# Adding up a norm's squares on GpSimd instead of VectorE, in a two-layer decoder trunk

## The chip, the core and the metric

One of the eight cores of a Trainium2 chip runs the whole program. The metric is the device time of one execution, in microseconds (us), taken as the median of several runs. The engines are called as in the profile: PE (TensorE), PEld (its weight loads), ACT (ScalarE), DVE (VectorE), POOL (GpSimd) and SP (SyncE, which only issues transfers here).

## What is computed

Two layers (`DEPTH` = 2) of a decoder trunk with model width 1024 are run on 592 tokens at once: 64 of the sample group, 16 meta tokens and 512 of the prompt. Cut to what matters here:

```python
def rmsnorm(x, g):
    xf = x.astype(jnp.float32)
    y = xf * lax.rsqrt(jnp.mean(xf * xf, axis=-1, keepdims=True) + EPS)
    return (y * g.astype(jnp.float32)).astype(x.dtype)

def swiglu(x, wg, wu, wd):
    return (jax.nn.silu(x @ wg) * (x @ wu)) @ wd

# one layer
h = h + 0.5 * swiglu(rmsnorm(h, norm_ffn1), ffn1_gate, ffn1_up, ffn1_down)
x = rmsnorm(h, norm_mix)
...                     # four mixers (convolution, retention, GLA, attention), gated and merged
h = h + merged @ w_out
h = h + 0.5 * swiglu(rmsnorm(h, norm_ffn2), ffn2_gate, ffn2_up, ffn2_down)
```

Each layer has three norms. Each needs, for every token, the sum of the squares of 1024 channels.

## The kernel before

The residual stream `hT` lies in SBUF as eight tiles (`KD` = 8) of 128 channels by 592 tokens. For a norm, ACT squares one tile into `tmp[:, 0, :]`; DVE adds this to `ssum` (128 by 592, float32); after eight tiles PE multiplies `ssum` by a matrix of ones, which adds over the partitions, and ACT makes the inverse root from it. `tmp[:, 0, :]` is one buffer: ACT may square tile m+1 only when the sum of tile m is done. Three semaphores carry this: `squared` (ACT has squared), `squares_summed` (the add is done) and `sum_cleared` (DVE has set `ssum` to zero).

All float32 operands of PE are split into a high and a low part (`x_hi`, `x_lo`, `w_hi`, `w_lo`); ACT writes the high parts, DVE the low ones, and PE makes three products of each pair. The gate and up projections are done as a fast matrix product of seven block products over halves of the operands, so for them sums and differences of halves of `hT` are formed as well (`T1`, `T2`, `T3`, `T4`, and the plain halves `B11`, `B22`, `B21`). This is done tile by tile as soon as a tile of `hT` is there: tiles 0 to 3 by `first_tile`, tiles 4 to 7 by `second_tile`, followed for the second FFN of a layer by `fourth` and the low parts of `T3`, `B21` and `T4`. The same engines also prepare, between the tiles, the weights for the first block products of the next stage (`first_operands`).

There are five places where tiles are squared for a gate and up projection:
- the prologue, on the input `h_in`, before the loop over layers (the add is at L2482)
- in each layer, `residual(l, 8, U_OUT, ...)`: `hT` is updated by the output projection (L2001, directly from PSUM), units of one weight block per tile, called the out stage below (adds at L1834)
- in each layer, `residual(l, 16, U_DOWN2, ...)`: `hT` is updated by the down projection of the second FFN (L1998, then L2001), three weight blocks per tile, called the down stage (adds at L1834). After layer 1 it is the last thing the kernel does, and nothing uses its squares.

The third norm of a layer, in front of the mixers, has its adds at L1974 and is not touched.

Every engine runs its own list of instructions in order and waits on semaphores. In the prologue ACT waits for `squares_summed` of the tile before, in front of the high part of the next tile; in `residual` it waits in `tile_added`, in front of the last weight unit of the next tile. PE waits for all eight adds in `norm`, which stands behind two block products of the first pair of the FFN (L1240). POOL's list in this kernel holds transfers alone: constants at the start, then one that waits for `brow` (`bias_row_made`, L569), caches and tables of the mixers within the loop, and at the end of a layer's list the parameters of the next layer (L661), which wait for the last low part `T4` of the second FFN.

Of the kernel before, what the change touches and what calls it, by code (L numbers as in the profile page):

```python
# [23 lines left out]
ALU = mybir.AluOpType  # L24
# [6 lines left out]
KD, KF = D // P, FF // P  # L31
# [29 lines left out]
KH = KD // 2  # L61
# [35 lines left out]
def parts(L, f, name, k):  # L97

    return L * sum(map(len, PARTS)) + f * len(PARTS[0]) + PARTS[f].index((name, k)) + 1
# [17 lines left out]
P_GAIN = 0  # L117
# [39 lines left out]
def split_cols(ap):  # L157

    return ap.rearrange("p (h t) -> p h t", h=2)


def build(nc, h_in, wstream, wlow, params, vbias, cache_k, cache_v, page_table, st_ret, st_gla,
# [9 lines left out]
    with ExitStack() as ctx:  # L172
        def sem(name):
            return ctx.enter_context(nc.semaphore(name))
# [7 lines left out]
        def keep(name, shape, dt=F32):  # L182
            nonlocal at
            t = place(name, shape, dt, at)
            at += -(-4 * int(np.prod(shape[1:])) // 32) * 32
            return t
# [11 lines left out]
        tmp = keep("tmp", [P, 2, T])  # L198
# [3 lines left out]
        ssum = keep("ssum", [P, 2 * NB * (CK - 1 + NT)])[:, 0:T]  # L202
# [142 lines left out]
        def pair(p):  # L345
            return ps[:, 2 * p:2 * p + 2, 0:HALF]
# [11 lines left out]
        sum_cleared = sem("sum_cleared")  # L358
        squared = sem("squared")
        squares_summed = sem("squares_summed")  # L360
# [193 lines left out]
        def _(pl):  # L554
            def load_values(l, p):

                for b in (2 * p, 2 * p + 1):
                    for pg in range(PAGES):
                        page = pl.value_load(pages[0:1, b * PAGES + pg:b * PAGES + pg + 1], min_val=0, max_val=POOL - 1)
                        pl.dma_start(vpage[:, b % 2, pg, :], cache_v[ds(l * POOL + page, 1)].rearrange("a p n -> (a p) n")).then_inc(values_loaded[b % 2], 16)  # L560

            pl.dma_start(prm[:, :], params[0][:, 0:NP_ - P]).then_inc(params_loaded, 16)
            pl.dma_start(pages[:, :], page_table).then_inc(consts_loaded, 16)
            pl.dma_start(ones[:, :, :], c_ones).then_inc(consts_loaded, 16)
# [1 line left out]
            pl.dma_start(coef[:, 0:2], c_coef).then_inc(consts_loaded, 16)  # L566
            pl.dma_start(rb[0:33, :], rel_bias).then_inc(consts_loaded, 16)
            pl.dma_start(bucket[0:33, :], c_bucket).then_inc(consts_loaded, 16)
            pl.wait_ge(bias_row_made, 3)  # L569
            pl.dma_start(scratch, brow[:, :]).then_inc(bias_row_stored, 16)  # L570
            pl.wait_ge(bias_row_stored, 16)
# [5 lines left out]
            with pl.Fori(0, DEPTH) as l:  # L577
# [77 lines left out]
                pl.dma_reset(range(nums[0], nums[-1] + 1))  # L655
                pl.sem_clear(range(nums[0], nums[-1] + 1))
                pl.sem_inc(mixers_open, 1)

                pl.wait_ge(x_parts, parts(l, 1, "T4", 3))
                pl.sem_inc(phases_entered, 1)  # L660
                pl.dma_start(prm[:, :], params[ds(l + 1, 1), :, 0:NP_ - P].rearrange("a p n -> (a p) n")).then_inc(params_loaded, 16)  # L661
            pl.wait_ge(params_loaded, 16 * (DEPTH + 1))


# [1071 lines left out]
        def _(v):  # L1736
# [5 lines left out]
            def unit_done(quad, slot):  # L1742
                v.wait_ge(units_multiplied, 4 * quad + slot + 1 + RING)
# [83 lines left out]
                else:  # L1827
                    v.scalar_tensor_tensor(lo, src, gain, hi.bitcast(F32), ALU.mult, ALU.subtract).then_inc(x_parts, 1)

            def square_sum(n):  # L1830

                v.wait_ge(squared, n + 1)
                v.wait_ge(squares_summed, n)
                v.tensor_tensor(ssum, ssum, tmp[:, 0, :], ALU.add).then_inc(squares_summed, 1)  # L1834

            def gain_of(gain, m):
                return prm[:, gain + m:gain + m + 1]

            def first_tile(L, f, k, gain, sum_squares):

                if k:
                    v.wait_ge(x_parts, parts(L, f, "T1", k - 1))
                v.tensor_tensor(tmp[:, 1, 0:HALF], hT[:, k, HALF:T], hT[:, k, 0:HALF], ALU.subtract).then_inc(x_parts, 1)
                x_low_of(L, f, "B11", k, hT[:, k, 0:HALF], gain_of(gain, k))
                sum_squares()
                v.wait_ge(x_parts, parts(L, f, "t1", k))
                x_low_of(L, f, "T1", k, tmp[:, 1, 0:HALF], gain_of(gain, k))

# [5 lines left out]
                v.wait_ge(x_parts, parts(L, f, late + "t3", k))  # L1854
                v.scalar_tensor_tensor(t2, hT[:, k, 0:HALF], gain_of(gain, k), t3, ALU.mult, ALU.add).then_inc(x_parts, 1)

            def second_tile(L, f, k, gain, sum_squares):

                differences(L, f, "", k, gain, tmp[:, 1, 0:HALF], tmp[:, 1, HALF:T])
                x_low_of(L, f, "B22", k, hT[:, KH + k, HALF:T], gain_of(gain, KH + k))  # L1860
                x_low_of(L, f, "T2", k, tmp[:, 1, 0:HALF], None)
                sum_squares()

            def fourth(L, f, late, k, gain, t2, t4):

# [111 lines left out]
            def residual(l, r0, first, units, scale, gain):  # L1977
                f = r0 % 16 // 8
                L, st = (l, l * 2 + 1) if f else (l + 1, l * 2 + 2)

                for m in range(KD):
                    r = l * 24 + r0 + m
                    k = m - KH

                    def sum_squares():
                        square_sum(8 + r)

                    for u in range(units):
                        pos = m * units + u
                        quad, slot = l * QUADS + first // RING + pos // RING, pos % RING  # L1990
                        if u == units - 1:
                            unit_done(quad, slot)
                            tile = split_cols(hT[:, m, :])
                            product = pair(OUT_PAIRS[m % 4])
                            if r0 == 16 and m:
                                v.wait_ge(x_parts, parts(L, 0, "T1", m - 1) if m <= KH else parts(L, 0, "T2", k - 1))
                            if r0 != 8:
                                v.tensor_tensor(split_cols(tmp[:, 1, :]), product, split_cols(inverse), ALU.mult).then_inc(out_scaled, 1)  # L1998
                                v.wait_ge(out_scaled, l * 16 + r0 // 2 + m + 1)
                                product = split_cols(tmp[:, 1, :])  # L2000
                            v.scalar_tensor_tensor(tile, product, scale, tile, ALU.mult, ALU.add).then_inc(residual_added, 1)  # L2001
                        if r0 and pos >= KD * units - RING:
                            if pos < KD * units - 1:
                                first_operands(st * KF, quad + 1, slot)
                            if r0 == 16 and m == KD - 1 and u == 1:
                                unit_done(quad, slot)
                                for n in range(2):
                                    late_third(L, n, gain)
                                    late_others(L, n, gain)
                        else:  # L2010
                            split_low(quad + 1, slot)
                    v.wait_ge(residual_added, r + 5)
                    if r0 == 0:
                        v.wait_ge(squared, 9 + r)
                        v.wait_ge(squares_summed, 8 + r)
                        v.wait_ge(x_high, l * 16 + m + 1)
                        sum_and_split(tmp[:, 0, :], hT[:, m, :], prm[:, gain + m:gain + m + 1], x_hi[:, m, :], x_lo[:, m, :])
                    elif m < KH:
                        first_tile(L, f, m, gain, sum_squares)
                    else:  # L2020
                        second_tile(L, f, k, gain, sum_squares)
                        if f and m < KD - 1:
                            fourth(L, f, "", k, gain, tmp[:, 1, 0:HALF], diff_rooms[:, k % 2, 2, :])
                            x_low_of(L, f, "T3", k, tmp[:, 1, HALF:T], None)
                            others_low(L, f, k, gain, diff_rooms[:, k % 2, 2, :])
                        if m == KD - 1:
                            first_operands(st * KF, quad + 1, RING - 1)
# [441 lines left out]
            for m in range(KD):  # L2469
                if m % 2 == 0:  # L2470
                    v.wait_ge(h_loaded[m // 2], 16)
                if m == KD - 1:
                    for n in range(2):
                        late_third(0, n, P_GAIN)
                        late_others(0, n, P_GAIN)

                def sum_squares():

                    v.wait_ge(squared, m + 1)
                    if m:  # L2480
                        v.wait_ge(squares_summed, m)
                    v.tensor_tensor(ssum, ssum, tmp[:, 0, :], ALU.add).then_inc(squares_summed, 1)  # L2482

                if m < KH:
                    first_tile(0, 0, m, P_GAIN, sum_squares)
                else:
                    second_tile(0, 0, m - KH, P_GAIN, sum_squares)
                if m % 2:
                    first_operands(0, 0, m // 2)
                if m == 5:  # L2490

                    v.wait_ge(consts_loaded, 16 * CONSTS)
                    v.tensor_scalar(rb[0:32, :], rb[0:32, :], 1.0 / ATT_SCALE, None, ALU.mult).then_inc(bias_row_made, 1)
# [207 lines left out]
```

## Time and profile before

| | |
|---|---|
| time, median of 3 runs | 3085.59 us (3084.69 to 3086.44) |
| profiled execution, own time | 3083.14 us |
| profiled execution, span | 3081.6 us |
| PE busy | 2937.7 us (95%) |
| DVE busy | 2087.4 us (68%) |
| ACT busy | 1284.2 us (42%) |
| POOL busy | 121.0 us (4%) |

The span is the time from the first to the last instruction that the profiler saw. A busy share is an average over the whole span: an engine with 68% can still be what all others wait for in one short stretch, and only the waits of this stretch tell.

### The profile page before, as it was taken

The numbers are of one execution on the slowest core, as the hardware profiler recorded it, in microseconds if no ns is written. First come the engines' busy times: TensorE is split into PE (matmuls) and PEld (weight loads), VectorE is DVE, ScalarE is ACT, GpSimd is POOL, SyncE is SP. The second block draws the span as 40 slices with busy tenths as digits, with TensorE's granted clock in tenths as the row PEclk, the third lists the DMA queues.
The fourth block names the chain that finished last, engine by engine and source line by source line (L and its number), as shares of the span: only waits on it lengthen the run. The fifth ranks groups of instructions, "written<-read, shape, count | busy, mean of one in ns | idle before, by whom it ended". The sixth has DMA issues, their size and how long they took to land.

```text
span 3081.6 us, 60278 instructions
## 1 busy us (share of the span) xinstructions
PE 2937.7 (95%) x21360; PEld 2794.3 (91%) x21360; DVE 2087.4 (68%) x3658; ACT 1284.2 (42%) x2206; POOL 121.0 (4%) x219
## 2 busy tenths in 40 slices
PE   4999999999899999999989999999998999999998
PEld 3999999888778989999989999998877889999998
DVE  7999534566556668996489983436665465799955
ACT  5556323334215245554255552233342242555533
POOL 0000001220000000000000000103100000000000
PEclk9999999999889999999999999999998899999999
DMA  3222224552213412223212232436412133122232
GB/s 112 96 94 97 96 86 160 170 183 72 83 58 125 155 48 92 87 95 105 88 56 95 95 103 89 148 107 198 139 66 92 64 141 129 56 96 87 99 99 89
DMA packets 102121, 319.61 MB, mean 104 GB/s; under 512 B 13503, under 2 KB 30063, under 8 KB 100272
## 3 DMA queue, kind: packets, MB, share of 16 engines
q1 hardware_dynamic: 89424, 275.82, 26.1%
q0 software_dynamic: 12512, 41.43, 4.2%
q8 instruction: 104, 1.70, 0.2%
q14 instruction: 81, 0.66, 0.1%
HBM read 290.02 MB, written 28.51 MB: 103 GB/s over the span
## 4 chain that ended last, share of the span: by engine, by line
PE 88%; DVE 5%; issue 3%; ACT 3%; DVEq 0%; DMA 0%; ACTq 0%; POOLq 0%
PE ps L1223 45%; PE ps L1252 32%; PE ps L1383 3%; PE ps L1476 1%; PE ps L1634 1%; PE ps L1235 1%; PE ps L1499 1%; PE ps L1513 1%; PE ps L1459 0%; ACT hT L1010 0%; DVE w_lo L1740 0%; PE ps L1514 0%; PE ps L1534 0%; ACT w_hi L711 0%; DVE x_more L1826 0%
## 5 line engine op out<-in xcount | busy, mean ns | idle before, releaser
L1740 DVE TENSOR_TENSOR w_lo<-w_raw,w_hi 128x1024 fp32r<-128x1024 f32 x240 | 292.7, 1223 | 397.1 <-ACT w_hi L671 391.8
L1252 PE MATMUL ps<-x_more,w_hi 128*128 128x296 f32 x2112 | 461.0, 300 | 11.1 <-DVE p_copy L1896 10.2
L671 ACT ACTIVATE w_hi<-w_raw 128x1024 fp32r<-128x1024 f32 x224 | 235.6, 1054 | 530.1 <-PE ps L1223 198.2
L1252 PE MATMUL ps<-x_hi,w_hi 128*128 128x296 f32 x1408 | 425.7, 302 | 26.5 <-ACT p_copy L775 14.9
L1252 PE MATMUL ps<-x_hi,w_lo 128*128 128x296 f32 x1408 | 424.9, 302 | 0.0
L1252 PE MATMUL ps<-x_lo,w_hi 128*128 128x296 f32 x1408 | 424.4, 301 | 0.0
L711 ACT ACTIVATE w_hi<-w_raw 128x512 fp32r<-128x512 f32 x445 | 272.2, 629 | 304.4 <-PE ps L1252 187.0
L1223 PE MATMUL ps<-x_hi,w_hi 128*128 128x296 f32 x1600 | 379.2, 319 | 13.1 <-ACT hT L1010 7.7
L1252 PEld LDWEIGHTS ps<-x_more,w_hi 128*128 128x128 f32 x2112 | 352.8, 189 | 12.4 <-issue 11.1
L1223 PE MATMUL ps<-x_hi,w_lo 128*128 128x296 f32 x1600 | 357.2, 305 | 0.0
L1223 PE MATMUL ps<-x_lo,w_hi 128*128 128x296 f32 x1600 | 356.4, 305 | 0.0
L1778 DVE TENSOR_TENSOR w_lo<-w_raw,w_hi 128x512 fp32r<-128x512 f32 x445 | 305.5, 687 | 29.0 <-ACT w_hi L711 22.7
L1252 PE MATMUL ps<-x_more,w_lo 128*128 128x296 f32 x1056 | 316.1, 299 | 0.0
L1223 PE MATMUL ps<-hid_hi,w_hi 128*128 128x296 f32 x1408 | 308.0, 300 | 2.6 <-DVE hid_lo L1936 2.6
L1223 PE MATMUL ps<-hid_hi,w_lo 128*128 128x296 f32 x1408 | 305.4, 298 | 0.0
L1223 PE MATMUL ps<-hid_lo,w_hi 128*128 128x296 f32 x1408 | 305.0, 298 | 0.0
L1223 PEld LDWEIGHTS ps<-x_hi,w_hi 128*128 128x128 f32 x1600 | 265.1, 195 | 41.5 <-issue 27.4
L1252 PEld LDWEIGHTS ps<-x_hi,w_hi 128*128 128x128 f32 x1408 | 269.2, 191 | 28.4 <-issue 28.2
L1252 PEld LDWEIGHTS ps<-x_hi,w_lo 128*128 128x128 f32 x1408 | 269.3, 191 | 0.4 <-issue 0.3
L1223 PEld LDWEIGHTS ps<-x_hi,w_lo 128*128 128x128 f32 x1600 | 269.2, 195 | 0.0
L1223 PEld LDWEIGHTS ps<-x_lo,w_hi 128*128 128x128 f32 x1600 | 268.2, 194 | 0.0
L1252 PEld LDWEIGHTS ps<-x_lo,w_hi 128*128 128x128 f32 x1408 | 268.0, 190 | 0.0
(344 smaller groups left out, 5016.2 us busy)
## 6 DMA issues: line engine op xcount, KB each, us to landing
w_raw<-wstream SPq DMA_DIRECT2D x420, 512.0 KB, 3.7
kpage<-cache_k SPq DMA_DIRECT2D x128, 128.0 KB, 2.8
vpage<-cache_v POOLq DMA_DIRECT2D x128, 128.0 KB, 3.1
gate_rows<-hT SPq DMA_DIRECT2D x48, 296.0 KB, 2.1
d_sg<-gate_rows SPq DMA_DIRECT2D x16, 888.0 KB, 4.6
hT<-h_in SPq DMA_DIRECT2D x4, 592.0 KB, 8.3
h_rows<-hT SPq DMA_DIRECT2D x2, 1184.0 KB, 5.4
hT<-h_rows SPq DMA_DIRECT2D x2, 1184.0 KB, 9.3
```

The lines of the kernel that those rows point to most:

```text
L671: act.activation(w_hi[:, slot, :, :], w_raw[:, slot, :, :], ACT.Copy).then_inc(weights_high, 1)
L711: act.activation(w_half(t)[0], w_source(t, g, total), ACT.Copy).then_inc(operands_high, 1)
L1223: mm = pe.matmul(ps[:, 2 * p + half, 0:HALF], wp[:, k, :], xp[:, k0 + k - blocks[0], half * HALF:(half + 1) * HALF], start=start and k == ...
L1235: mm = pe.matmul(ps[:, 2 * p + half, 0:HALF], mat, tile[:, half * HALF:(half + 1) * HALF], start=start, stop=stop)
L1252: mm = pe.matmul(ps[:, bank, 0:HALF], wp[:, k, :], xp, start=new and k == 0 and n == 0, stop=k == KH - 1 and n == 2, skip_group_check=True)
L1383: mm = pe.matmul(ps[0:n, (WINDOWS * g + w) % 8, 0:256], xp[:, k, c0:c0 + n], wp[:, s0:s0 + 2, k, :], start=k == 0 and m == 0, stop=k == KD ...
L1476: pe.matmul(ps[r0:r0 + 64, 5, 0:256], s_turn[:, s, r0:r0 + 64], vpage[:, r0 // 64, s, :], start=s == 0, stop=False)
L1499: mm = pe.matmul(ps[0:n, 2 * i, 0:min(ns, 512)], q, k[:, 0:min(ns, 512)], start=True, stop=True)
L1513: pe.matmul(out, V[:, s + 1, vc:vc + 64], p_turn[:, x % 2, s * P:(s + 1) * P], start=s == 0, stop=False)
L1634: mm = pe.matmul(ps[0:cols, h, 0:cols], k[:, c0:c0 + cols], q[:, c0:c0 + cols], start=True, stop=True)
L1740: v.tensor_tensor(w_lo[:, slot, :, :], w_raw[:, slot, :, :], w_hi[:, slot, :, :].bitcast(F32), ALU.subtract).then_inc(weights_low, 1)
L1778: v.tensor_tensor(lo, w_source(t, g, total), hi.bitcast(F32), ALU.subtract).then_inc(weight_steps, 1)
```

## The change

The adds at L2482 and L1834 leave DVE's list and go into POOL's. DVE no longer waits for `squared` there. The wait of each add for the one before it stays, now on POOL, and POOL waits for `sum_cleared` before the first add of each norm. ACT's and PE's waits for `squares_summed` stay as they are. The squares, their order and the sum are the same. 40 adds move: 8 in the prologue and 16 in each layer.

```diff
             pl.dma_start(bucket[0:33, :], c_bucket).then_inc(consts_loaded, 16)
+            pl.wait_ge(sum_cleared, 1)
+            for m in range(KD):
+                if m:
+                    pl.wait_ge(squares_summed, m)
+                sum_squares(m)
             pl.wait_ge(bias_row_made, 3)
...
+            def sum_squares(n):
+
+                pl.wait_ge(squared, n + 1)
+                pl.tensor_tensor(ssum, ssum, tmp[:, 0, :], ALU.add).then_inc(squares_summed, 1)
...
                 pl.sem_inc(mixers_open, 1)
+                pl.wait_ge(sum_cleared, 3 * l + 3)
+                for m in range(KD):
+                    pl.wait_ge(squares_summed, l * 24 + 16 + m)
+                    sum_squares(l * 24 + 16 + m)
 
                 pl.wait_ge(x_parts, parts(l, 1, "T4", 3))
                 pl.sem_inc(phases_entered, 1)
                 pl.dma_start(prm[:, :], params[ds(l + 1, 1), :, 0:NP_ - P].rearrange("a p n -> (a p) n")).then_inc(params_loaded, 16)
+                pl.wait_ge(sum_cleared, 3 * l + 4)
+                for m in range(KD):
+                    pl.wait_ge(squares_summed, l * 24 + 24 + m)
+                    sum_squares(l * 24 + 24 + m)
...
-            def square_sum(n):
-
-                v.wait_ge(squared, n + 1)
-                v.wait_ge(squares_summed, n)
-                v.tensor_tensor(ssum, ssum, tmp[:, 0, :], ALU.add).then_inc(squares_summed, 1)
...
                 x_low_of(L, f, "B11", k, hT[:, k, 0:HALF], gain_of(gain, k))
-                sum_squares()
                 v.wait_ge(x_parts, parts(L, f, "t1", k))
...
                 x_low_of(L, f, "T2", k, tmp[:, 1, 0:HALF], None)
-                sum_squares()
...
-                def sum_squares():
-
-                    v.wait_ge(squared, m + 1)
-                    if m:
-                        v.wait_ge(squares_summed, m)
-                    v.tensor_tensor(ssum, ssum, tmp[:, 0, :], ALU.add).then_inc(squares_summed, 1)
```

## Rows read from the trace of the kernel before

**Rows 1.** The page, busy time, share and count of each engine.

```profile
PE 2937.7 (95%) x21360; PEld 2794.3 (91%) x21360; DVE 2087.4 (68%) x3658; ACT 1284.2 (42%) x2206; POOL 121.0 (4%) x219
```

**Rows 2.** Waits, 0 to 62 us: engine, instruction <- releaser, total, times, longest.

```profile
PE ps L1252 <- DVE brow L2495: 9.9, 1, 9.9
...
ACT x_hi L720 <- DVE ssum L2482: 1.4, 3, 0.6
```

**Rows 3.** Instructions on `ssum`: durations in ns, first and last start.

```profile
L1834 DVE TENSOR_TENSOR ssum<-ssum,tmp x32: 765/773/777, 1105.3 to 3076.5; 128x592 f32<-128x592 f32 x32
...
L2482 DVE TENSOR_TENSOR ssum<-ssum,tmp x8: 767/774/776, 8.0 to 38.1; 128x592 f32<-128x592 f32 x8
```

**Rows 4.** Timeline of DVE in the prologue: start, duration, line, operation.

```profile
8.04 0.78 DVE L2482 TENSOR_TENSOR ssum<-ssum,tmp 128x592 f32<-128x592 f32 x1
8.74 0.52 DVE L1828 SCALAR_TENSOR_TENSOR x_lo<-tmp,prm,x_hi 128x296 fp32r<-128x296 f32 x1
...
38.15 0.78 DVE L2482 TENSOR_TENSOR ssum<-ssum,tmp 128x592 f32<-128x592 f32 x1
38.84 0.69 DVE L1778 TENSOR_TENSOR w_lo<-w_raw,w_hi 128x512 fp32r<-128x512 f32 x1
39.44 1.35 DVE L2495 COPY brow<-ps 16x1159 f32<-16x1159 f32 x1
```

**Rows 5.** Timeline of ACT in the prologue.

```profile
7.33 0.68 ACT L1177 ACTIVATE tmp<-hT 128x592 f32<-128x592 f32 x1
...
8.86 0.54 ACT L720 ACTIVATE x_hi<-hT,prm 128x296 fp32r<-128x296 f32 x1 [0.41 <-DVE ssum L2482]
```

**Rows 6.** Timeline of DVE in layer 0's out stage, tiles 1 and 4.

```profile
1107.74 0.77 DVE L2001 SCALAR_TENSOR_TENSOR hT<-ps,hT 128x592 f32<-128x592 f32 x1 [1.23 <-PE ps L1223]
...
1133.84 0.47 DVE L1826 TENSOR_TENSOR x_lo<-tmp,x_hi 128x296 fp32r<-128x296 f32 x1
1134.43 0.78 DVE L1834 TENSOR_TENSOR ssum<-ssum,tmp 128x592 f32<-128x592 f32 x1
1135.12 0.52 DVE L1867 SCALAR_TENSOR_TENSOR diff_rooms<-hT,prm,tmp 128x296 f32<-128x296 f32 x1
1135.56 0.46 DVE L1826 TENSOR_TENSOR x_more<-tmp,x_more 128x296 fp32r<-128x296 f32 x1
...
1136.75 0.77 DVE L2001 SCALAR_TENSOR_TENSOR hT<-ps,hT 128x592 f32<-128x592 f32 x1
```

**Rows 7.** Timeline of ACT in the same stretch.

```profile
1133.71 0.68 ACT L890 ACTIVATE tmp<-hT 128x592 f32<-128x592 f32 x1
...
1134.64 0.53 ACT L720 ACTIVATE x_more<-hT,prm 128x296 fp32r<-128x296 f32 x1
...
1137.83 0.63 ACT L711 ACTIVATE w_hi<-w_raw 128x512 fp32r<-128x512 f32 x1 [1.70 <-DVE hT L2001]
```

**Rows 8.** Timeline of PE at the end of this out stage.

```profile
1155.77 0.61 PE L1252 MATMUL ps<-x_hi,w_hi 128*128 128x296 f32 x1 [5.51 <-ACT p_copy L775]
```

**Rows 9.** Timeline of DVE at the end of layer 0's down stage.

```profile
1550.06 1.30 DVE L1778 TENSOR_TENSOR w_lo<-w_raw,w_hi 128x512 fp32r<-128x512 f32 x2 [3.89 <-ACT w_hi L711]
...
1560.88 0.78 DVE L1834 TENSOR_TENSOR ssum<-ssum,tmp 128x592 f32<-128x592 f32 x1
1561.58 0.69 DVE L1778 TENSOR_TENSOR w_lo<-w_raw,w_hi 128x512 fp32r<-128x512 f32 x1
1564.67 0.53 DVE L1853 SCALAR_TENSOR_TENSOR diff_rooms<-hT,prm,side 128x296 f32<-128x296 f32 x1 [2.41 <-ACT side L763]
```

**Rows 10.** End of the kernel: timeline of SP, and that transfer's size and landing.

```profile
3074.12 0.35 SPq L547 DMA_DIRECT2D y_out<-hT  x1
...
y_out<-hT SPq DMA_DIRECT2D x1, 2368.0 KB, 7.0
```

**Rows 11.** The page, costliest groups: the same form of instruction at 1024 and 512 columns.

```profile
L1740 DVE TENSOR_TENSOR w_lo<-w_raw,w_hi 128x1024 fp32r<-128x1024 f32 x240 | 292.7, 1223 | 397.1 <-ACT w_hi L671 391.8
...
L1778 DVE TENSOR_TENSOR w_lo<-w_raw,w_hi 128x512 fp32r<-128x512 f32 x445 | 305.5, 687 | 29.0 <-ACT w_hi L711 22.7
```

**Rows 12.** Groups of instructions on POOL: its longest instructions.

```profile
L610 POOL DMA_DIRECT2D convs_out<-ue_s x4 | 3.6, 904 | 14.8 <-issue 14.8
```

More of the change, by code:

```diff
@@ L1828, in x_low_of, with first_tile @@
                     v.scalar_tensor_tensor(lo, src, gain, hi.bitcast(F32), ALU.mult, ALU.subtract).then_inc(x_parts, 1)
-            def square_sum(n):
-                v.wait_ge(squared, n + 1)
-                v.wait_ge(squares_summed, n)
-                v.tensor_tensor(ssum, ssum, tmp[:, 0, :], ALU.add).then_inc(squares_summed, 1)
             def gain_of(gain, m):
                 return prm[:, gain + m:gain + m + 1]
-            def first_tile(L, f, k, gain, sum_squares):
+            def first_tile(L, f, k, gain):
                 if k:
@@ L1855, in differences, with second_tile @@
                 v.scalar_tensor_tensor(t2, hT[:, k, 0:HALF], gain_of(gain, k), t3, ALU.mult, ALU.add).then_inc(x_parts, 1)
-            def second_tile(L, f, k, gain, sum_squares):
+            def second_tile(L, f, k, gain):
                 differences(L, f, "", k, gain, tmp[:, 1, 0:HALF], tmp[:, 1, HALF:T])
@@ L1983, in residual @@
                     k = m - KH
-                    def sum_squares():
-                        square_sum(8 + r)
                     for u in range(units):
@@ L2018, in residual @@
                     elif m < KH:
-                        first_tile(L, f, m, gain, sum_squares)
+                        first_tile(L, f, m, gain)
                     else:
-                        second_tile(L, f, k, gain, sum_squares)
+                        second_tile(L, f, k, gain)
                         if f and m < KD - 1:
@@ L2475, in _ @@
                         late_others(0, n, P_GAIN)
-                def sum_squares():
-                    v.wait_ge(squared, m + 1)
-                    if m:
-                        v.wait_ge(squares_summed, m)
-                    v.tensor_tensor(ssum, ssum, tmp[:, 0, :], ALU.add).then_inc(squares_summed, 1)
                 if m < KH:
-                    first_tile(0, 0, m, P_GAIN, sum_squares)
+                    first_tile(0, 0, m, P_GAIN)
                 else:
-                    second_tile(0, 0, m - KH, P_GAIN, sum_squares)
+                    second_tile(0, 0, m - KH, P_GAIN)
                 if m % 2:
```

## The prediction, made before the changed kernel ran

> **What bounds the kernel now.** I read the busy shares first. PE is busy 95% of the span and DVE 68% [rows 1], so work taken from DVE is worth something only in the few stretches where PE stands still. The views of `ssum` then say where the 40 adds lie: 8 between 8 and 38 us, 32 from 1105 us on, each 0.77 us long [rows 3]. On DVE the next instruction starts 0.69 us after the start of an add (8.04 to 8.74, 38.15 to 38.84) [rows 4]; 0.69 is thus what an add takes from a busy DVE. Then I went through the five places one by one, with the waits and the timelines.
>
> *Prologue.* PE waits 9.9 us for DVE's copy `brow`, which stands at the end of DVE's prologue list [rows 2], so all of this list is on the path. DVE runs there almost without a gap. But ACT runs a loop with it: it squares tile m, waits for the add, and starts tile m+1. The square of tile 0 ends at 7.33 + 0.68 = 8.01, the add at 8.82, and ACT goes on at 8.86, having stood 0.41 us [rows 4, 5]; in all it stood 3 times, 1.4 us, for an add [rows 2]. The two engines are nearly in balance.
>
> *Out stages.* For tile 1 DVE still waits 1.23 us for PE before it updates `hT`; for tiles 1 to 4 PE leads. The update of tile 5 at 1136.75 has no idle time before it [rows 6], and so have those of tiles 6 and 7: DVE is behind, and it is the list of DVE and ACT that sets the pace. It is paid at the end: PE stands 5.51 us until ACT has worked its way to a copy that PE needs [rows 8]. So the adds of tiles 4, 5 and 6 are on the path, in both layers: 6 adds. That of tile 7 comes after the values that ACT waits for.
>
> *Down stages.* DVE has idle time behind the add of tile 6 (3.89 us) and behind that of tile 7 (2.41 us) [rows 9]. At the end of the kernel the store of `y_out` goes out at 3074.12 and lands 7.0 us later [rows 10]; the last add comes only after it was issued, at 3076.5 [rows 3].
>
> **The change, part by part.** *Removed from DVE:* 8 × 0.69 = 5.5 us in the prologue and 6 × 0.69 = 4.1 us in the out stages, if nothing else held these places. The other 26 adds lie under PE or beside idle time and free nothing.
>
> *Added on POOL:* the same add, 40 times. No row shows POOL computing. It can't well be shorter than on DVE, 0.77 us [rows 3]. For a longer one I take an engine that reads its two inputs one after the other: 2 × 592 = 1184 columns. DVE needs 1.22 us for 1024 and 0.69 us for 512 columns [rows 11], so (1.223 − 0.687)/512 = 1.05 ns a column, and 1.22 + 160 × 1.05 = 1.39 us; its copy of 1159 columns took 1.35 us [rows 4]. As the upper end I put POOL's longest instruction on top, 1.39 + 0.90 = 2.3 us [rows 12]. I take 1.4 us, because it sits next to two rows. The Trainium skill (GPSIMD Engine Reference, Performance versus the Vector engine) has GpSimd about twice as slow as VectorE at this add, for the very reason that its two inputs share a read port; its figure of 4497 ns for 2048 columns would make 1.3 us here, an estimate, and the sum about 1.4 us smaller. No run here shows it yet.
>
> *What runs beside it.* In DVE's list nearly every instruction of these stretches reads two operands from SBUF (the rows of L1826, L1828, L1867, L1778 name two each [rows 4, 6]), and so does POOL's add. If the two engines must take turns at reading SBUF, then POOL's 1.4 us stand in DVE's way just as an add of DVE's own would, and longer. In an out stage: T2's low part ends at 1133.84 + 0.47 = 1134.31, `diff_rooms` follows to 1134.8, POOL then holds the port to 1136.2, and `T3`'s low part, at 1135.56 today, starts at 1136.2. That is 0.65 us late, and the update of the next tile with it [rows 6, 7]. Six times: +3.9 us. In the prologue I went through the list by hand with this rule, tile by tile: each add holds DVE 1.4 instead of 0.69 us and nothing catches up, because the next tile's `x_lo` waits for ACT, ACT for the add, and DVE has no gaps to give. It comes to 8 × 0.7 = +5.6 us, less 0.1 for the first tile. Together +9.4 us. The Trainium skill (SBUF — State Buffer, Who interferes with whom) says so of the hardware: a VectorE instruction with two SBUF inputs contends with a GpSimd instruction that reads SBUF, and whoever comes second waits for all of the first. This trace can neither confirm nor deny it, having no such pair.
>
> *Down stages:* 0.7 us more is covered by the 3.89 and 2.41 us of idle time [rows 9]. Were that cover gone, it would be 0.7 us for a tile. After the last add of layer 0's down stage DVE's `w_lo` at 1561.58 would move to about 1562.4 and end before 1564.67. At the end, the add of tile 7 would last until 3078, before 3074.12 + 7.0 = 3081.1: nothing.
>
> *POOL's queue:* the `bias_rows` store waits for `brow` anyway, which is later than the eighth add in either case. The parameters' transfer waits for `T4` of the second FFN, long after the adds of the out stage. Behind the adds of the down stage there is nothing until the next layer's mixers. PE's wait for eight adds stands behind two block products; PE starts the first of them at 1155.77, on a copy that ACT makes only after the square of tile 7 [rows 8], so an add that ends 1.5 us after this square is in time. I cost both at nothing.
>
> Sum: 3085.6 + 9.4 = 3095.0 us. The terms come from an execution of 3083.14 us, 0.08% under the median; the difference is added to the median, since it scales nothing.
>
> **The rivals.**
>
> *No taking turns.* POOL works freely beside DVE. Then an out stage gains what DVE saves: after 1134.31 DVE goes straight to `diff_rooms`, `T3`; `B21`'s low part waits for ACT's high part, which ends at 1134.64 + 0.53 = 1135.17 [rows 7]; the update of the next tile comes at 1136.02 instead of 1136.75, 0.73 us sooner. ACT's wait for POOL's add (1134.39 + 0.1 + 1.4 = 1135.9) is over before it wants to start its `w_hi`, which follows the end of the update by 0.3 us (1137.83 today), so at about 1137.1 [rows 6, 7]. Six times: −4.4 us. The prologue gains much less: ACT now goes on at 8.01 + 0.1 + 1.4 = 9.5 instead of 8.86, so the tiles that follow each other directly lose what DVE saves, and only where weights stand between tiles is something won. Through the list by hand this makes `brow` 0.9 us earlier. In all −5.3 us: 3080.3 us, not slower. For it speaks that nothing in this trace shows the two engines disturbing each other; against it, that the change puts them on the same memory at the same moment, 14 times on the path. It decides once POOL's add leaves DVE's neighbours at 0.46 to 0.53 us each and closely spaced. At POOL's upper price of 2.3 us ACT's loop in the prologue costs 8 × up to 0.4 us more, and the gain is about 2 us.
>
> *DVE always goes first.* The port is shared, but POOL gets it only when DVE has nothing to read. Then DVE loses nothing and the add ends late. In the out stage POOL starts at the update of the next tile (1136.0), ends at 1137.4, and ACT's `w_hi` comes 0.4 instead of 0.73 us earlier: −2.3 us over six. In the prologue ACT waits for the add, DVE for ACT, and POOL for DVE to run dry; some 0.8 us for each of eight tiles, +6. In all about +4 us: 3090 us.
>
> *The add is much dearer with turns taken.* At 2.3 us, (2.3 − 0.69) × 14 = +22 us; 3108 us. At 0.77 us, +1 us.
>
> **How the numbers follow.** Turns taken as in the forecast: 0.55, with its own range from +6 (an add of 1.1 us) to +15 us (1.8 us), 3092 to 3101 us. No turns: 0.25. DVE first: 0.15. Much dearer: 0.05. The range 3080 to 3101 us leaves out the dearest cases and the outer half of the gains, 2 in 10. What a measurement of this kernel can tell from no change is about 0.2%, 6.2 us. Slower by more than this: nearly all of the first and the last case above, less what falls under +6.2 us, 0.50. Faster by more: only the no-turns case with a gain above its own sum, for instance if PE, idle a shorter time, kept its clock: 0.08. Between: 0.42.
>
> **What the profile after would show.** POOL has 40 instructions on `ssum`, spaced or lasting about 1.4 us. Where they lie, instructions of DVE with two SBUF operands last 1 us or more longer than the 0.46 to 0.53 us of today, or start late without a wait. `brow` starts near 45 instead of 39.44 us. In the out stages the updates of tiles 5 to 7 come 0.65, 1.3 and 1.9 us later from the start of the stage, and PE's gap grows from 5.5 to about 7.5 us. The down stages keep their length. The prediction is wrong if DVE's durations stay as they are, or if ACT's wait for `ssum` in the prologue becomes the long one.

## The result, and the profile after

| | before | after |
|---|---|---|
| time, median of 16 runs each | 3084.62 us (3079.64 to 3086.93) | 3089.53 us (3087.15 to 3095.2) |
| ratio after to before | | 1.002 (1.0013 to 1.0027) |
| profiled execution, span | 3081.6 us | 3087.8 us |

By the ratio of 1.002 the change costs 6.2 us, with a 95% interval of +4.0 to +8.3 us; the two medians of the table differ by 4.9 us, which lies inside it. That is right at the 0.2% that I had called the limit of what can be told, and its interval leaves out zero. The two profiled spans differ by 6.2 us as well. The forecast was +9.4 us, with turns taken at the SBUF reads as the mechanism.

The page of the changed kernel, the row that answers to [rows 1]:

```profile
PE 2934.8 (95%) x21360; PEld 2793.1 (90%) x21360; DVE 2101.5 (68%) x3618; ACT 1283.2 (42%) x2206; POOL 180.5 (6%) x259
```

DVE has 40 instructions fewer than in [rows 1] and is busy 14 us more. 40 adds left it, each of which took 0.69 us of a full list and lasted 0.77, 28 to 31 us in all; so 42 to 45 us came back on instructions that nobody edited (a closer count against `write_twice`, below, gives 39). That is the first thing to see: the work went away and the time did not.

The instructions on `ssum`, durations in ns as least, median and most (against [rows 3]):

```profile
L565 POOL TENSOR_TENSOR ssum<-ssum,tmp x40: 1425/1473/1812, 8.2 to 3082.8; 128x592 f32<-128x592 f32 x40
```

The timelines of POOL, DVE, ACT and PE of the changed kernel in the prologue, one fence for each; columns are start, duration, line, operation, and in brackets the idle time before and what ended it:

```profile
8.16 1.43 POOL L565 TENSOR_TENSOR ssum<-ssum,tmp 128x592 f32<-128x592 f32 x1 [2.73 <-ACT tmp L1195]
...
15.13 1.81 POOL L565 TENSOR_TENSOR ssum<-ssum,tmp 128x592 f32<-128x592 f32 x1 [2.81 <-ACT tmp L1195]
```

```profile
8.54 1.37 DVE L1846 SCALAR_TENSOR_TENSOR x_lo<-tmp,prm,x_hi 128x296 fp32r<-128x296 f32 x1 [0.56 <-ACT x_hi L738]
...
14.98 0.68 DVE L1813 TENSOR_TENSOR w_raw<-gu,w_raw 128x512 f32<-128x512 f32 x1
15.69 1.80 DVE L1819 TENSOR_TENSOR gu<-w_raw 128x512 f32<-128x512 f32 x1
...
44.76 1.35 DVE L2495 COPY brow<-ps 16x1159 f32<-16x1159 f32 x1
```

```profile
9.62 0.54 ACT L738 ACTIVATE x_hi<-hT,prm 128x296 fp32r<-128x296 f32 x1 [1.18 <-POOL ssum L565]
```

```profile
46.70 0.61 PE L1270 MATMUL ps<-x_hi,w_hi 128*128 128x296 f32 x1 [11.30 <-DVE brow L2495]
```

POOL's first add runs from 8.16 to 9.59. DVE's `x_lo`, 0.52 us long in [rows 4], starts inside it at 8.54 and lasts 1.37 us: it ends 0.32 us after the add. The second add goes the other way round. It starts at 15.13, while DVE is inside L1813 (until 15.66), and it is the add that is stretched, to 1.81 us; DVE's next instruction, L1819, then waits for it and takes 1.80. Who has begun goes on, and the other waits. The waiting shows as a longer duration of the one that waits, and not as idle time. `brow` comes at 44.76 instead of 39.44, and PE starts 5.3 us later than the 41.39 of the kernel before.

The same in the out stage of layer 0 (POOL, then DVE, then PE), which answers to [rows 6] and [rows 8]:

```profile
1139.74 1.59 POOL L565 TENSOR_TENSOR ssum<-ssum,tmp 128x592 f32<-128x592 f32 x1 [9.00 <-ACT tmp L908]
```

```profile
1139.11 0.47 DVE L1844 TENSOR_TENSOR x_lo<-tmp,x_hi 128x296 fp32r<-128x296 f32 x1
1139.49 0.52 DVE L1877 SCALAR_TENSOR_TENSOR diff_rooms<-hT,prm,tmp 128x296 f32<-128x296 f32 x1
1140.04 1.62 DVE L1844 TENSOR_TENSOR x_more<-tmp,x_more 128x296 fp32r<-128x296 f32 x1
1141.58 0.52 DVE L1846 SCALAR_TENSOR_TENSOR x_more<-hT,prm,x_more 128x296 fp32r<-128x296 f32 x1
...
1142.39 0.76 DVE L2008 SCALAR_TENSOR_TENSOR hT<-ps,hT 128x592 f32<-128x592 f32 x1
...
1150.23 0.76 DVE L2008 SCALAR_TENSOR_TENSOR hT<-ps,hT 128x592 f32<-128x592 f32 x1
...
1158.06 0.76 DVE L2008 SCALAR_TENSOR_TENSOR hT<-ps,hT 128x592 f32<-128x592 f32 x1
```

```profile
1162.14 0.61 PE L1270 MATMUL ps<-x_hi,w_hi 128*128 128x296 f32 x1 [6.57 <-ACT p_copy L793]
```

One instruction of DVE, `T3`'s low part, takes 1.62 us; its neighbours take what they took. The updates of `hT` are 7.84 us apart. Before, they were 7.47 us apart, so each tile costs 0.37 us more. PE's gap grew from 5.51 to 6.57 us.

I measured all traces with the same four numbers: PE's start behind the prologue; the length of the out stage, from the first update of `hT` to PE's restart, for layer 0 / layer 1; the span; and the timed result against the kernel before on the same chip. "One run" is a single time, without an interval.

| kernel | PE start | out stages | span | timed |
|---|---|---|---|---|
| before | 41.39 | 54.57 / 54.62 | 3081.6 | |
| after | 46.70 | 55.73 / 55.74 | 3087.8 | 1.002 (1.0013 to 1.0027) |
| prologue only | 46.38 | 54.60 / 54.63 | 3084.2 | 1.0015 (1.0006 to 1.0024) |
| loop only | 41.32 | 55.79 / 55.77 | 3080.2 | 0.9997 (0.9988 to 1.0006) |
| down stages only | 41.46 | 54.64 / 54.65 | 3083.5 | 0.9999 (0.999 to 1.0008) |
| bystander | 48.91 | 57.32 / 57.38 | 3094.8 | 1.0051 (1.0035 to 1.0068) |
| write only | 39.53 | 52.56 / 52.57 | 3070.3 | 3072.07, one run (before: 3082.46) |
| write twice | 40.71 | 52.57 / 52.57 | 3074.9 | 3076.49, one run (before: 3082.72) |
| one input | 40.78 | 53.39 / 53.33 | 3076.6 | 3078.37, one run (before: 3082.46) |
| ungated | 41.59 | 55.58 / 55.56 | 3082.3 | 0.9998 (0.9989 to 1.0007) |
| gated | 41.16 | 52.81 / 52.72 | 3074.3 | 0.9971 (0.996 to 0.9982) |
| gate only | 41.61 | 54.74 / 54.66 | 3080.0 | 3081.5, one run (before: 3082.72) |

### The profile page after: what moved, and what is told of

Its sections match the earlier page's. It is cut to its first block, busy times and chain, and to the rows that moved or that the text cites. A ratio compares the mean times of both kernels' runs of the same rounds, so it can differ in the third digit from the quotient of the medians.

```text
span 3087.8 us, 60281 instructions
## 1 busy us (share of the span) xinstructions
PE 2934.8 (95%) x21360; PEld 2793.1 (90%) x21360; DVE 2101.5 (68%) x3618; ACT 1283.2 (42%) x2206; POOL 180.5 (6%) x259
## 4 chain that ended last, share of the span: by engine, by line
PE 86%; DVE 5%; issue 4%; ACT 3%; POOLq 0%; DMA 0%; POOL 0%; DVEq 0%; ACTq 0%
PE ps L1241 43%; PE ps L1270 31%; PE ps L1401 3%; PE ps L1652 1%; PE ps L1494 1%; PE ps L1253 1%; PE ps L1517 1%; PE ps L1531 1%; ACT hT L1028 0%; DVE w_lo L1758 0%; PE ps L1532 0%; ACT w_hi L729 0%; PE ps L1477 0%; PE ps L1552 0%; POOLq L559 0%
## 5 line engine op out<-in xcount | busy, mean ns | idle before, releaser
L1796 DVE TENSOR_TENSOR w_lo<-w_raw,w_hi 128x512 fp32r<-128x512 f32 x445 | 312.4, 703 | 32.7 <-ACT w_hi L729 26.7
```

Of the source, the lines that this page charges most:

```text
L1796: v.tensor_tensor(lo, w_source(t, g, total), hi.bitcast(F32), ALU.subtract).then_inc(weight_steps, 1)
```

## The experiments

**Where it sits: one part of the change at a time.** Against the changed kernel, `prologue_only` gives DVE the adds of the loop back and `loop_only` those of the prologue; `down_only` moves nothing but the adds of the down stages. The edits of `prologue_only` and of `loop_only`:

```diff
-                pl.wait_ge(sum_cleared, 3 * l + 3)
-                for m in range(KD):
-                    pl.wait_ge(squares_summed, l * 24 + 16 + m)
-                    sum_squares(l * 24 + 16 + m)
...
+            def square_sum(n):
+
+                v.wait_ge(squared, n + 1)
+                v.wait_ge(squares_summed, n)
+                v.tensor_tensor(ssum, ssum, tmp[:, 0, :], ALU.add).then_inc(squares_summed, 1)
```

```diff
-            pl.wait_ge(sum_cleared, 1)
-            for m in range(KD):
-                if m:
-                    pl.wait_ge(squares_summed, m)
-                sum_squares(m)
             pl.wait_ge(bias_row_made, 3)
...
+                def sum_squares():
+
+                    v.wait_ge(squared, m + 1)
+                    if m:
+                        v.wait_ge(squares_summed, m)
+                    v.tensor_tensor(ssum, ssum, tmp[:, 0, :], ALU.add).then_inc(squares_summed, 1)
```

> Only the 8 adds of the prologue go to POOL; the loop keeps its 32 on DVE. If the places add up as read from the trace of the changed kernel (brow 5.3 us later), this gives before + 5.3 us. Rival (the loss is in the out stages or spread over the loop): before + 0 to 1 us.

> Only the 32 adds of the loop go to POOL; the prologue keeps its 8 on DVE. From the trace of the changed kernel (1.1 us in each of two out stages): before + 2.3 us, with tiles 5 to 7 of the out stages 7.84 instead of 7.47 us apart and the down stages unchanged. Rival (the down stages pay as well): 16 more adds at 0.4 us, before + 6 to 9 us.

The traces separate cleanly. With the prologue's adds alone PE starts at 46.38 us and the out stages keep their 54.6 us; with the loop's alone PE starts at 41.32 and the out stages take 55.8 us. Timed, the prologue costs +4.6 us (+1.8 to +7.4) and the loop −0.9 us (−3.7 to +1.9). The loop's +1.2 us for each of two out stages is thus seen in the trace and not in the time; the interval just leaves out my expected +2.3. The last section comes back to this.

The down stages by themselves, against the kernel before:

```diff
+                pl.wait_ge(sum_cleared, 3 * l + 4)
+                for m in range(KD):
+                    pl.wait_ge(squares_summed, l * 24 + 24 + m)
+                    sum_squares(l * 24 + 24 + m)
...
-                        first_tile(L, f, m, gain, sum_squares)
+                        first_tile(L, f, m, gain, sum_squares if r0 == 8 else None)
...
-                        second_tile(L, f, k, gain, sum_squares)
+                        second_tile(L, f, k, gain, sum_squares if r0 == 8 else None)
```

> Only the 16 adds of the two down stages go to POOL. Theory (DVE has idle time behind each): before within 0.1%, the tiles 17.96 us apart as before, and the store of y_out issued as long after PE's restart of layer 1 as before (402.7 us). Rival (they pay too): before + 6 us.

It is the same as before within 0.1%. Idle time on DVE takes up what POOL's adds cost there, as two rows of the changed kernel show, which answer to [rows 9]:

```profile
1567.79 1.51 DVE L1796 TENSOR_TENSOR w_lo<-w_raw,w_hi 128x512 fp32r<-128x512 f32 x1 [0.64 <-ACT w_hi L729]
...
1571.29 0.53 DVE L1864 SCALAR_TENSOR_TENSOR diff_rooms<-hT,prm,side 128x296 f32<-128x296 f32 x1 [1.99 <-ACT side L781]
```

`w_lo` is stretched from 0.69 to 1.51 us, and DVE still stands idle for 1.99 us behind it.

**What it is: the reading, the wait or the engine.** Three kernels keep the changed kernel's semaphores and give POOL something else to do, so the sum of squares is missing or incomplete in them. `write_only` and `write_twice` read nothing; `one_input` reads one operand. The added `sem_inc(phases_entered, 1)` releases nobody. Edit of `write_only`, then of `one_input`:

```diff
-                pl.tensor_tensor(ssum, ssum, tmp[:, 0, :], ALU.add).then_inc(squares_summed, 1)
+                pl.sem_inc(phases_entered, 1)
+                pl.memset(ssum, 128.0).then_inc(squares_summed, 1)
```

```diff
-                pl.tensor_tensor(ssum, ssum, tmp[:, 0, :], ALU.add).then_inc(squares_summed, 1)
+                pl.sem_inc(phases_entered, 1)
+                pl.tensor_copy(ssum, tmp[:, 0, :]).then_inc(squares_summed, 1)
```

> The changed kernel, with POOL setting ssum to a constant where it added: the sum of squares is left out, the semaphores are the same. POOL writes 592 columns and reads nothing. Theory (turns at reading): no DVE instruction is stretched; DVE saves its adds; brow starts before 39.44 us, the updates of tiles 5 to 7 follow each other after about 6.7 us instead of 7.47, and the whole is 5 us or more under before. Rival (any POOL instruction on SBUF disturbs DVE): stretched DVE instructions beside the POOL ones, as in the changed kernel, shorter only as the POOL instruction is shorter.

> The changed kernel, with POOL copying the squares into ssum where it added: it reads one operand of 592 columns instead of two, and the sum of the other tiles is left out. Theory (the port is held for as long as POOL reads): POOL's instruction lasts about half of 1.43 us, DVE instructions beside it end 0.3 us after its end, stretched by about half as much as in the changed kernel; the time falls to that of before or 1 to 4 us under it. Rival (a fixed price for each meeting of the two engines): the stretch of about 0.9 us stays.

`write_only` puts no stretched instruction on DVE, and the kernel gets faster than before. But its 0.59 us is also shorter than the add, so ACT waits less, and that would fit the rival in which ACT's wait is what costs. `write_twice` was made to part the two: two memsets, one behind the other, keep ACT waiting as long as the add does and still read nothing.

```diff
-                pl.tensor_tensor(ssum, ssum, tmp[:, 0, :], ALU.add).then_inc(squares_summed, 1)
+                pl.sem_inc(phases_entered, 1)
+                pl.memset(ssum, 128.0).then_inc(ssum_set, 1)
+                pl.wait_ge(ssum_set, count)
+                pl.sem_inc(phases_entered, 1)
+                pl.memset(ssum, 128.0).then_inc(squares_summed, 1)
```

> The changed kernel with POOL setting ssum to a constant twice, the second after the first is done, where it added; the sum of squares is left out. One setting took 0.59 us, so a pair keeps ACT waiting about 1.4 us, as the add does, and reads nothing from SBUF. Theory (the prologue's loss is DVE blocked by POOL's reads): PE starts its first product at 40 to 41 us, before the 41.39 of the kernel before; my hand count gave 0.9 us sooner. Rival (the loss is ACT's wait for a slow add): near the 46.7 us of the changed kernel.

POOL, ACT and PE of `write_twice` in the prologue:

```profile
8.26 0.59 POOL L567 MEMSET ssum<- 128x592 f32 x1 [2.84 <-issue]
...
9.00 0.59 POOL L570 MEMSET ssum<- 128x592 f32 x1 [0.15 <-POOL ssum L567]
```

```profile
9.62 0.54 ACT L743 ACTIVATE x_hi<-hT,prm 128x296 fp32r<-128x296 f32 x1 [1.08 <-POOL ssum L570]
```

```profile
40.71 0.61 PE L1275 MATMUL ps<-x_hi,w_hi 128*128 128x296 f32 x1 [9.52 <-DVE brow L2500]
```

ACT goes on at 9.62, to the hundredth where it does in the changed kernel, and PE starts at 40.71 instead of 46.70. With the same wait and no reads, the change would have gained 0.7 us in the prologue and 2.0 us in each out stage (52.57 against 54.57). So the reads cost 46.70 − 40.71 = 6.0 us in the prologue and 55.73 − 52.57 = 3.2 us in an out stage. ACT's longer wait costs something too, but only in the prologue: with one memset in place of two PE starts at 39.53 us, 1.2 us sooner than in `write_twice`, while the out stages are the same (52.56 and 52.57 us). DVE's busy time says what one add holds: 2101.5 us in the changed kernel against 2062.2 in `write_twice` with the same 3618 instructions, 39.3/40 = 0.98 us for each add. For `one_input` it is (2071.8 − 2062.2)/40 = 0.24 us; a row of DVE and the copy beside it:

```profile
1131.78 0.72 POOL L566 COPY ssum<-tmp 128x592 f32<-128x592 f32 x1 [9.49 <-ACT tmp L909]
```

```profile
1131.98 0.83 DVE L1845 TENSOR_TENSOR x_more<-tmp,x_more 128x296 fp32r<-128x296 f32 x1
```

0.83 instead of 0.46 us: one input is enough for a conflict. It is a smaller one than I had expected: POOL's copy lasts half as long as the add, and the mean stretch is a quarter of the add's (0.24 of 0.98 us), not half.

**The other way round: a bystander.** DVE keeps its own adds, as before the change, and POOL adds two operands that nobody needs, at the same moments, in the prologue and in the out stages (24 adds).

```diff
+            def bystander(n, done):
+
+                pl.wait_ge(squared, n + 1)
+                pl.wait_ge(idle_done, done)
+                pl.tensor_tensor(idle_out, idle_tile, idle_tile, ALU.add).then_inc(idle_done, 1)
...
+            for m in range(KD):
+                bystander(m, m + 1)
...
+                for m in range(KD):
+                    bystander(l * 24 + 16 + m, l * 8 + 9 + m)
...
+                v.wait_ge(idle_done, (l + f) * 8 + 9)
                 if f == 0:
```

> The kernel before, with its adds on DVE, and beside them on POOL one add of 592 columns of zeros for each square of the prologue and of the out stages, into a place that nothing reads. Nobody waits for it before the next FFN begins. Theory (the two engines take turns at reading SBUF): DVE instructions that fall into a POOL add last about 1.4 us instead of 0.5 to 0.8; each of the 14 adds on the path costs what POOL holds the port, 1.1 to 1.4 us, with nothing saved: 15 to 20 us more than before. Rival (the cost of the change is ACT's wait for a slow add): POOL's add releases nobody here, so the time is that of before within 0.2%, and no DVE instruction is longer.

POOL and DVE of `bystander`:

```profile
8.19 1.75 POOL L570 TENSOR_TENSOR hid<-idle 128x592 f32<-128x592 f32 x1 [2.61 <-ACT tmp L1192]
```

```profile
8.83 1.43 DVE L1843 SCALAR_TENSOR_TENSOR x_lo<-tmp,prm,x_hi 128x296 fp32r<-128x296 f32 x1
...
10.30 1.35 DVE L1858 TENSOR_TENSOR tmp<-hT 128x296 f32<-128x296 f32 x1
```

Only POOL's adds were put in, and the kernel is 15.7 us slower (+10.8 to +21 us). DVE looks once in a stage, long after the last of them, that they are done; the trace shows no wait for them. The second row, 1.35 us for a `tmp` of 0.46, starts after the first add's end (9.94), so it stands beside the next one. The trace has +7.5 us in the prologue and +2.75 us in each out stage, 13.0 us for the 14 adds on the path: 0.93 us each, under the 1.1 to 1.4 us that I had expected. DVE's busy time grows by 24.3 us, 1.01 us for each of 24. A further 1.5 us lies between PE's restart in layer 1 and the store of `y_out` (404.20 against 402.74 us), where no bystander add runs beyond the first microseconds; I give it no cause.

**Can the gain be had?** `write_twice` had shown that 2.0 us lie in each out stage. The update of `hT` reads one operand from PSUM and one from SBUF, and ACT's next product is far away at that point; if the add is made to lie beside it, nothing may be in its way. `ungated` (from `loop_only`) takes ACT's wait for `squares_summed` out of `tile_added` in the out stage and puts it in front of the next square, so that the add may be late; `gated` adds a wait that holds POOL until DVE has made `T4`'s low part, which is followed by the update. The edit of `ungated`, and what `gated` has beside it:

```diff
                     def square():
+                        act.wait_ge(squares_summed, r + 8)
                         act.activation(tmp[:, 0, :], hT[:, m, :], ACT.Square).then_inc(squared, 1)
 
                     def tile_added():
                         act.wait_ge(residual_added, r + 1 + 4)
-                        act.wait_ge(squares_summed, r + 8)
+                        if r0 == 0:
+                            act.wait_ge(squares_summed, r + 8)
```

```diff
                     pl.wait_ge(squares_summed, l * 24 + 16 + m)
+                    if KH <= m < KD - 1:
+                        pl.wait_ge(x_parts, parts(l, 1, "T4", m - KH))
                     sum_squares(l * 24 + 16 + m)
```

> The same as the gated kernel without POOL's wait for T4; only ACT's wait for the add has moved, in the loop. Theory (DVE is blocked, ACT's wait costs nothing in the out stages): the time of the kernel with the loop's adds alone on POOL, before + 2.3 us. Rival (the cost was ACT's wait in front of the weight unit): like the gated one, under before.

> As the kernel with the loop's adds alone on POOL, but in the out stages POOL waits, for tiles 4 to 6, until the low part of T4 is done, so that its add lies beside the update of hT (one operand in PSUM, one in SBUF) and DVE's wait for ACT (0.98 us); ACT's wait for the add moves from the weight unit of the next tile to just before the next square. Theory (only a DVE instruction with two SBUF operands meets POOL's reads): the update is not stretched, each tile saves 0.73 us, tiles 5 to 7 come 6.7 us apart, before - 4.4 us. Rival (an update with one SBUF operand is stretched as well): it lasts 1.6 us or more and the gain is gone, before + 0 to 4 us.

DVE, POOL and PE of `gated` in layer 0's out stage:

```profile
1134.97 0.77 DVE L2011 SCALAR_TENSOR_TENSOR hT<-ps,hT 128x592 f32<-128x592 f32 x1
...
1136.64 0.69 DVE L1795 TENSOR_TENSOR w_lo<-w_raw,w_hi 128x512 fp32r<-128x512 f32 x1 [0.91 <-ACT w_hi L726]
```

```profile
1135.21 1.47 POOL L565 TENSOR_TENSOR ssum<-ssum,tmp 128x592 f32<-128x592 f32 x1 [10.90 <-DVE x_more L1843]
```

```profile
1152.91 0.40 PE L1269 MATMUL ps<-x_hi,w_hi 128*128 128x296 f32 x1 [3.66 <-ACT p_copy L790]
```

The add starts at 1135.21, in the middle of the update, and neither is longer for it: 0.77 and 1.47 us. Behind `diff_rooms`, which reads two SBUF operands, the add of the changed kernel had taken 1.59 us. The rest of it lies in 0.91 us of DVE's idle time. The updates are now 6.67 us apart instead of 7.47, and PE's gap is 3.66 us instead of 5.51. `gated` is faster than the kernel before, and so than the changed one: 3074.56 us (3071.56 to 3075.84) against 3082.74 us, by the ratio −8.9 us (−12.3 to −5.5), by the medians −8.2 us. `ungated` alone stands at no change in time, where I had expected +2.3 us; its out stages are 1.0 us longer than before, with updates 7.75 to 7.77 us apart.

That is about twice the 4.4 us I had expected; the out stages give 54.57 − 52.81 and 54.62 − 52.72, 3.7 us. Part of the rest comes behind PE's restart. Windows of 8 us that begin 0.77 and 0.91 us before it, columns as us, busy time of PE, PEld, DVE, ACT and POOL with counts, PE's granted clock, DMA share and GB/s; the kernel before, then `gated`:

```profile
1155.00:1163.00 8.00, 7.23 (x29) 6.59 (x29) 5.04 (x10) 4.42 (x10) 0.54 (x1) 0.57 0.38 133
```

```profile
1152.00:1160.00 8.00, 7.09 (x37) 6.45 (x38) 6.20 (x10) 5.42 (x11) 2.01 (x2) 0.79 0.40 141
```

In these windows PE did 37 matmuls at a mean granted clock of 0.79 in `gated`, and 29 at 0.57 in the kernel before, much nearer to the lower of its two levels (1.2 of 2.4 GHz). From the restart to PE's second wait it took 12.11 instead of 13.13 us: 1.0 us for each restart, 2.0 us in both layers. That the clock is what gives this 1.0 us is not shown. In `bystander` PE's gap was 8.26 us, and in the 8 us from its restart on it did 43 matmuls at 0.78, as many as `gated` (43 at 0.79; before: 34 at 0.61); it still took 13.14 us to the second wait, because DVE was late with a `p_copy` (2.10 us of waiting). So neither does a longer gap always bring the lower clock, nor does the higher clock always bring the second wait forward. With the 3.7 us that makes 5.7, inside the interval of the timing; what makes up the remaining 3 us of its middle I did not find.

Is it the gate by itself? `gate_only` has POOL's wait, but leaves ACT's wait where it was:

```diff
+                for m in range(KD):
+                    pl.wait_ge(squares_summed, l * 24 + 16 + m)
+                    if KH <= m < KD - 1:
+                        pl.wait_ge(x_parts, parts(l, 1, "T4", m - KH))
+                    sum_squares(l * 24 + 16 + m)
```

> The gated kernel with ACT's wait for the add back in front of the weight unit of the next tile. POOL's add ends about 1.7 us after the start of the update, ACT would go on 1.0 us after it, so ACT waits 0.7 us more: tiles 5 to 7 of the out stages come 7.3 us apart (gated: 6.67; before: 7.47), and an out stage is 0.5 us shorter than before instead of 1.8. Rival (ACT's wait does not matter there): 6.67 us, as gated.

ACT of `gate_only`:

```profile
1136.63 0.63 ACT L726 ACTIVATE w_hi<-w_raw 128x512 fp32r<-128x512 f32 x1 [2.46 <-POOL ssum L565]
```

The updates are 7.60 us apart and the out stage takes 54.74 us, against 54.57: the late add now stands in ACT's way, 2.46 us here. I had expected 7.3 and a small gain. This is one run and its trace, but with `ungated` it says that the gain needs both edits: an add that disturbs nobody, and nobody who waits for it.

## Why the prediction was right, step by step

- *The price of an add on POOL*, forecast 1.4 us: the median is 1.47, and 1.43 where DVE isn't in its way. The estimate from columns read one input after the other was right within 0.1 us; the estimate scaled from the figure of the Trainium skill (GPSIMD Engine Reference, Performance versus the Vector engine) was 1.3 us, and the measured one lies a little above that.
- *Turns taken at the SBUF reads*, the likeliest case at 0.55: shown. Stretched neighbours, the first that reads going first in either direction, nothing of it with POOL writing only, and all of it with a bystander that nobody waits for. The Trainium skill (SBUF — State Buffer, Who interferes with whom) has the second one wait for all of the first; the trace agrees on the order. The delay of DVE is smaller than the add's recorded 1.47 us: 0.98 us by the busy times, 0.93 us by the bystander. In part that is because DVE often comes late to it: `x_lo` of the prologue started 0.38 us into the add and lost 0.85 us, while an instruction of the out stage that started 0.07 us into it, at 1109.70, lasted 1.73 instead of 0.46 us and so lost 1.27.
- *Prologue*, forecast +5.5 us: +5.3. The number is right, but its parts are not, and that is luck. The forecast had each add hold DVE 0.7 us longer than before and gave DVE no gaps. From the start of its list to `brow`, DVE's busy time grew from 31.00 to 33.01 us only, and its idle time from 1.6 to 4.9 us: 3.3 of the 5.3 us are DVE standing idle for ACT, which itself goes on later behind each add (its first wait for `ssum` was 1.18 instead of 0.41 us). The add that holds less than forecast and the gaps that were put at nothing cancel.
- *Out stages*, forecast +0.65 us a tile and +3.9 us in all: +0.37 us a tile, +1.16 and +1.12 us a stage, 2.3 us. This is the term of the sum that was mis-sized. I had put the add's start behind `diff_rooms` and let it hold DVE for its full 1.4 us. It starts while `diff_rooms` runs, 0.63 us after the start of `T2`'s low part, and `T3`'s low part ends at 1141.66, 1.62 instead of 0.46 us long. Taking off its own 0.46 us, DVE could go on at 1141.20: 1.19 us after the end of `diff_rooms` (1140.01), where the forecast had 1.4, and 0.13 us before the recorded end of the add. So the hold was mis-sized, at 1.4 for 1.19 us. PE's gap became 6.57 and not 7.5 us.
- *Down stages, the kernel's end, POOL's queue*, forecast nothing: restart of layer 1 to the store of `y_out` is 402.74 us in both, and `down_only` is the same as before.
- *Sum:* 5.3 + 2.3 = 7.6 us by these places, 6.2 us in the span. Between the restart of layer 0 (+6.4 us) and the first update of layer 1 (+5.1 us) the changed trace gains 1.3 us, after the down stage of layer 0, in the first FFN and the mixers of layer 1, which the change doesn't touch. In the twelve traces this stretch lasts from 1459.4 to 1464.5 us (1461.0 before, 1459.7 after), so I give it no cause.
- *The rivals.* "No taking turns" was wrong for this kernel, and right for what would be without the reads: forecast −0.9 us in the prologue and −0.73 us a tile, while `write_twice` shows −0.7 and −0.72. "DVE always first" was wrong: DVE waits as soon as POOL has begun. Its 3090 us is nearer to the measured 3089.53 than any other forecast, and the measured time lies under the range of the case that came true (3092 to 3101 us); by the time alone the wrong one would have been picked, and only the rows tell them apart. "Much dearer": no.
- *The chances.* "Within 0.2%" got 0.42 and "slower" 0.50; the result lies on the border between them.

## What to carry to other kernels

Work moved from DVE to POOL doesn't leave DVE when both read SBUF: before moving it, look at what DVE runs at that moment, because its two-operand instructions stretched here by two thirds of POOL's instruction on the mean (0.98 of 1.47 us), which was more than the 0.69 us saved. It pays where POOL's instruction can be placed beside a DVE instruction that reads PSUM, or beside idle time, and where nobody waits for it; both conditions have to be made, by a wait on POOL and by moving the consumer's wait. A busy time that grows on an engine whose list got shorter is the sign of it on the page.

## What the hardware showed that I had not expected

- A DVE instruction with one operand in PSUM and one in SBUF and POOL's add ran beside each other undisturbed. In `gated` and `gate_only` this happened 12 times: the update lasted 0.76 or 0.77 us, as alone, and the add 1.43 to 1.48 us. The update had always begun first, by 0.24 or 0.25 us, so what is shown is that it doesn't hold the add; an update that begins inside an add is in no trace. This is what made `gated` possible. A DVE instruction with two SBUF operands that came behind a later update of the same kernel was held:

```profile
1149.28 1.04 DVE L1865 SCALAR_TENSOR_TENSOR tmp<-hT,prm,side 128x296 f32<-128x296 f32 x1 [0.21 <-DVE hT L2011]
```

  It took 1.04 us, against 0.52 us when nothing is beside it.
- Three microseconds that belong to no edit. The retention stage of layer 0, a stretch that no experiment touches, takes about 38.4 us in five of the traces (before, after, `ungated`, `gated`, `write_twice`) and about 35.6 us in the other seven. In layer 1 it is `down_only` alone that takes 38.4 us. Before and after agree within 0.5 us in both layers, so the 6.2 us between their spans don't come from it. Windows of the kernel before and of `loop_only` there, columns as above:

```profile
796.00:805.00 9.00, 8.36 (x72) 7.19 (x72) 1.18 (x2) 2.23 (x6) 0.00 (x0) 0.54 0.07 26
```

```profile
796.00:805.00 9.00, 8.20 (x104) 7.17 (x104) 1.22 (x3) 2.48 (x6) 0.00 (x0) 0.69 0.09 34
```

  PE is busy alike in both and does 72 matmuls in one and 104 in the other; the granted clock is 0.54 and 0.69. So two single spans can differ by 2.8 us in a stretch without an edit. It is nearly the size of what is missing between `loop_only`'s out stages (+2.4 us in the trace) and its time (−0.9 us); that it is the cause there is not shown. Whether a kernel has one or the other for good, or each execution by itself, stays open: there is one trace of each kernel. This is why I read the out stages from the traces, stage by stage, and the verdicts from the timed runs.
